# Modulation rows of a two-model block: four row pieces of 512 columns against two halves of 256 columns times even and odd channel tiles

## The reference, cut to what matters

```
s_lat = jax.nn.silu(c)[:, None, :]
s_ctx = jax.nn.silu(c_ctx)
for l in range(DEPTH):                                  # DEPTH = 2
    ml = jnp.split(s_lat @ w_mod[l] + b_mod[l], N_MOD, axis=-1)   # N_MOD = 9
    mc = jnp.split(s_ctx @ w_mod[l] + b_mod[l], N_MOD, axis=-1)
    x = half_ffn(x, g_norm[l, 0], ml[0], ml[1], ml[2], ...)
```

## Time and profile before

| | |
|---|---|
| median of 3 runs | 3228.5 us (3228.48 to 3229.98) |
| the profiled execution's own time | 3231.32 us |
| its span | 3230.0 us |
| mean granted TensorE clock over the span | 0.983 of full speed |
| TensorE matmul busy | 3072.6 us, 95% |
| TensorE weight load busy | 2408.0 us, 75% |
| VectorE, ScalarE, GpSimd busy | 1209.6, 595.6 and 50.5 us |
| read from memory | 366.96 MB |

### The profile page before, as it was taken

One profiled execution on the slowest core, in us unless ns is written; L12 is line 12 of the kernel. 1 busy time (PEld: TensorE's weight loads), 2 busy tenths in 40 slices (PEclk: granted clock), 3 DMA queues, 4 the chain that ended last, 5 costly groups with the idle time before them and its releaser, 6 DMA issues.

```text
span 3230.0 us, 38678 instructions
## 1 busy us (share of the span) xinstructions
PE 3072.6 (95%) x16538; PEld 2408.0 (75%) x16538; DVE 1209.6 (37%) x2504; ACT 595.6 (18%) x1314; POOL 50.5 (2%) x78
## 2 busy tenths in 40 slices
PE   7879989999899989999999898999989999999999
PEld 5656678888588868888844447888878888755888
DVE  3265433213523125445222625445244453235100
ACT  1232212112412021000022621100011000224100
POOL 0000000002000000000000000000000000000000
PEclk9989999999999999999999999999999999999999
DMA  6339964456244442222212102222323223231443
GB/s 218 127 138 327 327 212 143 130 171 170 79 133 138 124 156 66 91 62 72 88 65 62 53 29 76 79 78 68 102 78 97 78 54 85 93 99 53 131 132 103
DMA packets 355822, 370.50 MB, mean 115 GB/s; under 512 B 7395, under 2 KB 282228, under 8 KB 355524
## 3 DMA queue, kind: packets, MB, share of 16 engines
q1 hardware_dynamic: 350224, 358.04, 35.0%
q0 software_dynamic: 2208, 5.31, 0.9%
q10 hardware_dynamic: 3220, 4.68, 0.4%
HBM read 366.96 MB, written 1.05 MB: 114 GB/s over the span
## 4 chain that ended last, share of the span: by engine, by line
PE 91%; DVE 4%; ACT 3%; issue 1%; DMA 1%; ACTq 0%; POOL 0%; DVEq 0%
PE acc L130 77%; PE aux L130 13%; ACT sb_xn L263 1%; PE aux L2054 1%; DVE sb_big L1355 0%; ACT sb_work L1372 0%; DMA weights<-mix_w_in 0%; ACT sb_work L1374 0%; DMA sb_x<-xT 0%; DVE sb_work L1573 0%; DVE sb_work L1570 0%; PE aux L1496 0%; ACT sb_rstd L254 0%; DVE sb_work L2200 0%; ACT sb_rstd L256 0%
## 5 line engine op out<-in xcount | busy, mean ns | idle before, releaser
L130 PE MATMUL acc<-sb_xn,weights 128*128 128x256 f32 (+1 forms) x5360 | 1309.0, 400 | 47.3 <-ACT sb_xn L263 34.3
L130 PEld LDWEIGHTS acc<-sb_xn,weights 128*128 128x128 f32 x5360 | 1019.5, 191 | 297.5 <-issue 161.3
L130 PE MATMUL acc<-sb_big,weights 128*128 128x256 f32 x2040 | 448.3, 379 | 0.0
L130 PEld LDWEIGHTS acc<-sb_big,weights 128*128 128x128 f32 x2040 | 387.6, 190 | 53.2 <-issue 0.4
L130 PE MATMUL acc<-sb_work 128*128 128x256 f32 x1320 | 308.4, 379 | 0.0
L130 PE MATMUL acc<-sb_work,weights 128*128 128x256 f32 (+4 forms) x1104 | 285.9, 404 | 6.1 <-DVE sb_work L1144 6.0
L130 PEld LDWEIGHTS acc<-sb_work 128*128 128x128 f32 x1320 | 250.8, 190 | 37.9 <-issue 4.3
L130 PEld LDWEIGHTS acc<-sb_work,weights 128*128 128x128 f32 (+2 forms) x1104 | 205.2, 187 | 66.9 <-issue 39.4
L1850 DVE TENSOR_TENSOR sb_work<-sb_work,acc 128x256 f32<-128x256 f32 x78 | 32.8, 421 | 260.1 <-PE acc L130 260.1
L130 PE MATMUL aux<-sb_xn,sb_work 128*128 128x256 f32 x528 | 126.0, 382 | 0.0
L1236 DVE SCALAR_TENSOR_TENSOR sb_work<-acc,sb_cols,sb_work 128x255 f32<-128x255 f32 x88 | 42.5, 482 | 195.0 <-ACT sb_work L1224 195.0
(11 more groups left out here) (302 smaller groups left out, 2638.4 us busy)
## 6 DMA issues: line engine op xcount, KB each, us to landing
weights<-ffn_w_up SPq DMA_DIRECT2D x88, 1024.0 KB, 7.9
weights<-w_mod SPq DMA_DIRECT2D x36, 2048.0 KB, 9.2
weights<-ffn_w_down SPq DMA_DIRECT2D x48, 1408.0 KB, 7.0
weights<-ffn_w_gate SPq DMA_DIRECT2D x44, 1024.0 KB, 5.4
weights<-w_in SPq DMA_DIRECT2D x8, 2048.0 KB, 8.3
weights<-mix_w_in SPq DMA_DIRECT2D x6, 2048.0 KB, 13.5
weights<-na_w_qkv SPq DMA_DIRECT2D x6, 2048.0 KB, 8.1
weights<-ple_w_gate SPq DMA_DIRECT2D x4, 2048.0 KB, 7.9
```

What stands on the lines that cost most here:

```text
L130: return te.matmul(o, lhsT, rhs, start=start, stop=stop, skip_group_check=True)
```

## The change

The work of the four array quarters is cut in another way. A quarter t now takes only half of the block's columns (256 of them, half t // 2) and only every other k tile (the even ones for even t, the odd ones for odd t). It has four k tiles over 256 columns, where it had two over 512. The bank then holds, in its columns 0 to 255, four rows: two halves of columns times two partial sums. ScalarE copies 256 columns. `pick` becomes 128x4, and a column product of 128 row columns gives four output columns (two halves of columns, two conditions), so a block has two column products. VectorE reads the eight columns of the bank in their new order. Everything that waits or signals stays where it was.

```diff
-    sil, pick = area(work, 12416, KT, 32), area(work, 12672, 2)
+    sil, pick = area(work, 12416, KT, 32), area(work, 12672, 2, 2)
...
-        pick_set.on(ve.tensor_reduce(pick, ident[:].rearrange("p (j s) -> p s j", s=32)[:, 0:2, :], AX.X, ALU.add))
+        pick_set.on(ve.tensor_reduce(pick, ident[:].rearrange("p (n j s) -> p n s j", n=2, s=32)[:, :, 0:2, :], AX.X, ALU.add))
...
         def columns(j):
             g, row = mod_blocks[j][2].groups[0], mod_rows[j % 2]
             te.wait_ge(mod_row.sem, mod_row_at(j))
-            for c in range(4):
-                ins_ = mm(acc[g.bank][:, 2 * c:2 * c + 2], row[:, 128 * c:128 * c + 128], pick)
+            for c in range(2):
+                ins_ = mm(acc[g.bank][:, 4 * c:4 * c + 4], row[:, 128 * c:128 * c + 128], area(work, 12672, 4))
             mod_cols.on(ins_)
...
-            for q in range(4):
-                mm(acc[g.bank][32 * q:32 * q + 32, :], sil[:, q, :], w[:, q, :], True, False)
+            for q in range(8):
+                k, t = 2 * (q // 4) + q % 2, q % 4
+                mm(acc[g.bank][32 * t:32 * t + 32, 0:256], sil[:, k, :], w[:, k, 256 * (t // 2):256 * (t // 2) + 256], q < 4, False)
             yield
             if j:
                 columns(j - 1)
-            for q in range(4):
-                ins_ = mm(acc[g.bank][32 * q:32 * q + 32, :], sil[:, 4 + q, :], w[:, 4 + q, :], False, True)
+            for q in range(8):
+                k, t = 4 + 2 * (q // 4) + q % 2, q % 4
+                ins_ = mm(acc[g.bank][32 * t:32 * t + 32, 0:256], sil[:, k, :], w[:, k, 256 * (t // 2):256 * (t // 2) + 256], False, q >= 4)
             acc_full.on(ins_)
...
-            mod_row.on(ac.copy(mod_rows[j % 2][:, :], acc[g.bank][:, :]))
+            mod_row.on(ac.copy(mod_rows[j % 2][:, 0:256], acc[g.bank][:, 0:256]))
...
             acc_free[g.bank].on(ve.tensor_tensor(
-                mod[:, at:at + 4, :], acc[g.bank][:, 0:8].rearrange("p (n s) -> p n s", s=2),
-                cols("b_mod", 4, at).unsqueeze(2).to_broadcast([128, 4, 2]), ALU.add))
+                mod[:, at:at + 4, :].rearrange("p (n c) s -> p c n s", n=2), acc[g.bank][:, 0:8].rearrange("p (c n s) -> p c n s", c=2, n=2),
+                cols("b_mod", 4, at).rearrange("p (n c) -> p c n", n=2).unsqueeze(3).to_broadcast([128, 2, 2, 2]), ALU.add))
```

## The result

The changed kernel takes 3234.8 us (median of 22 runs, 3230.4 to 3242.4), the kernel before 3230.1 us on the same chips (22 runs). The ratio is 1.0015, 95% interval 1.0009 to 1.0022: slower by 4.7 us, where 3212.9 was forecast. TensorE's stream did become shorter as worked out. It then stood still for want of instructions: the gain went into waits for its instruction fetch. In the views such a stall is marked "issue", which is time in which TensorE waits for no semaphore that the profile shows.

A forecast was written before the change was run, and what follows sets the result against it. The prediction took the length of TensorE's stream to bound the recurrence; -15.7 (column products) + 0.7 (half blocks) - 0.6 (row copy) = -15.6 us, so 3228.5 - 15.6 = 3212.9 us, range 3209.5 to 3219.5.

The forecast's parts named there:

- What bounds the kernel: Recurrence, 200 to 433 us: bound by the length of TensorE's stream, busy 225.9 of 233 us; other engines' work covered.
- Column products: Modulation on TensorE: four records instead of eight save 0.45 us a block, 35 times, 15.7 us less.
- Half blocks: Modulation on TensorE: four rounds of 256 columns instead of two of 512 add 0.01 us each, 72 times, +0.7 us.
- the rival of open weight loads: Half blocks: added rounds expose their weight loads; 3216.3 us if loaded at once (chance 0.12), 3228.6 in turn (0.04).
- Row copy: ScalarE's copy of the bank's rows falls from 0.57 to 0.38 us; TensorE's waits for it go, -0.6 us.
- Covers and transfers: Recurrence: VectorE's and ScalarE's work and w_mod loads stay hidden, 0 us; rivals: short cover (chance 0.07), transfers as bound (0.05).
- Instructions: TensorE's stream in the recurrence: 864 added records, 10%, and 3 to 4 more fetches; taken as 0, bounds -3 to +4 us.
- instruction fetch falls behind: Rival, half blocks and dense 64x64 products: all fetches stall at 1.25 us each, +41 us, 3254 us; chance 0.02.
- Its deciding point: Fetch rival in the recurrence: 12 additional stalls, from 15.6 / 1.25.
- the starting value: Whole kernel: time before the change taken as 3228.5 us, the profiled execution's 3231.3 less 2.8 for the median.
- Both signs that I had named for being wrong: The recurrence shrinking by less than 11 us, or something behind 433 us moving by more than 2.

The follow-up runs named there:

- e8: Kernel before, with four modulation blocks packed in one bank and a 128x8 picker, one column product for a block: 3219.0 us, ratio 0.9966.
- e11: e8 with its instruction boundaries moved by 64 idle instructions at TensorE's start: 3208.1 us, ratio 0.9931 to the kernel before.
- e7: Kernel before, with two modulation blocks packed in one bank, two column products for a block, 288 records fewer: 3212.4 us, ratio 0.9943.
- e3: Changed kernel with only two of eight k tiles of w_mod transferred: 3216.8 us, ratio 0.9953 to the kernel before.
- e6: Kernel before, with its instruction boundaries moved by 64 idle instructions at TensorE's start: 3240.9 us, ratio 1.0034.

## Why the prediction was wrong, by its own steps

- *What bounds the kernel.* Right that TensorE's stream sets the time of the stretch and that ScalarE and VectorE are covered. What I took for granted is the supply of its instructions.
- *Column products.* Forecast 0.45 us less for a block and some 20 us of busy time for all; measured 0.99 to 0.54 us, 22.2 us. Right.
- *Half blocks.* Forecast +0.01 us each; measured slots of 1.00 against 0.99. Right, and with it the rival of open weight loads fell: the x16 groups are 1.07 us. The Trainium skill ("TensorE: Matmul & The Clock Gate", section "What overlaps and what doesn't") has weight loads overlap only across row groups; these four quarters, which all use every row, don't follow it, and the measurement decides.
- *Row copy.* Forecast 0.38 us, measured 0.373, waits gone. Right.
- *Covers and transfers.* Right: no new wait, and landings take at most 10.7 us. e8 and e11 shorten the cover further and wait for neither.
- *Instructions.* **This step failed.** I scaled the 3.0 us of issue time with the number of records (+0.3), called the stalls few, took 0 and bounded it by -3 and +4. Measured are +12.4 us of issue idle time and 3.4 us for the clock after the two longest stalls, and the recurrence came out 2.2 us longer in place of 15.6 shorter. The remaining 2.0 us are 0.6 of added waits for L1070 and some tenths at stalls that the view doesn't mark. Two things were wrong. The cost of stalls does not scale with the number of records: 10% more records made five times the idle time. An estimate of the pace says where it set in: the kernel before takes its 8474 records of the recurrence at 36 for each us and the packed one (e7) at 38, while the forecast asked for 43 and 40 came. The same records passed at 43 in e3, with light queues. And the clock behind a stall was not in the sum at all. The hint stood in the profile of before: five such stalls in the stretch, and dense 64x64 work at 32 matmul and 32 load records in 1 us, one fetched piece in about 4 us.
- *The rivals.* The right one was among them, as "instruction fetch falls behind", with a chance of 0.02 and a price of +41 us. Its deciding point was 12 additional stalls; 14 came (19 against 5). Its price was too high: not every one of some 36 fetches stalled but 19, for 15.4 / 19 = 0.8 us of idle time each and not 1.25, so it ended at +22 over the forecast.
- *The size of the result.* The time is 21.9 us over the forecast. In the profiled pair 17.8 of them lie in the recurrence, and 1.6 are the starting value: the forecast began at 3228.5, and the kernel before took 3230.1 in its 22 runs. The rest is in parts that no run ties to the change. Both signs that I had named for being wrong came, the recurrence shrinking by less than 11 us and the part behind moving by more than 2 (it moved by 3.7); the second says nothing here, since that part moves by up to 3.2 in programs without the change. No step of mine considered that a program's time depends by 10 us on where its instructions lie.

What stays open: why a place is good or bad. Every stall ends with a fetch, but no run shows when a fetch is asked for, so I can't say which records must stand at a boundary, nor how long a fetch waits ahead of its packet.

## What to carry to other kernels

Count the records that a change adds to TensorE's stream, and where: in a stretch with short matmuls and full memory queues they are not free, and stalls marked "issue" there are the sign to look for. Compare the end of such a stall with the fetches on q8, and read the granted clock behind it, since the clock can cost as much as the stall. Prefer an edit that saves time by fewer instructions (here, packing two blocks into the idle columns of the stationary operand) to one that saves the same time with more. Before you judge a change of a few us in such a kernel, move both versions by some idle instructions at the start and compare the means.

## What was not expected of the hardware

64 idle instructions at TensorE's start changed a program's time from 3231.1 to 3240.9 us, and 128 changed the packed one from 3212.4 to 3228.0. TensorE goes on 1.2 to 1.8 us after a fetch has ended, at each of 123 stalls. A stall of 3.2 us in a stretch that was at full clock was followed by 3.4 us at half clock, and one of 2.2 us in e6 by 6.8 us. Four rounds of 256 columns in four array quarters side by side cost the same as two of 512 (1.07 against 1.06 us), twice the weight loads included. The transfers held 356 GB/s over 200 us, where the kernel before had 317.
